# First output projection by column halves, with decay exponents as differences of running totals, in a three-block model on one core

## The reference

```python
proj = h @ w_in                      # q, k, v, g_a, z, xbc, dt_raw
y_a = rmsnorm(diff_attention(q, k, v), subln_w) * silu(g_a)
dt = softplus(dt_raw + dt_bias)      # 512 tokens x 16 heads
dA = dt * -exp(a_log)                # in 4 chunks of 128 tokens
cs = cumsum(dA, axis=-1)             # running total within the chunk
lmat = exp(where(l >= s, cs[l] - cs[s], -inf))
cb = einsum('bclgn,bcsgn->bcgls', cc, bc)
y_diag = einsum('bcgjls,bcsgjp->bclgjp', cb * lmat, xdt)
states = einsum('bclgn,bcgjl,bclgjp->bcgjpn', bc, exp(cs[-1] - cs), xdt)
h = h * exp(cs[-1]) + states         # scan over the chunks
y_off = einsum('bclgn,bcgjpn,bcgjl->bclgjp', cc, h_before, exp(cs))
y_b = rmsnorm_by_groups((y_diag + y_off + xh * d_skip) * silu(z))
x = x + concatenate([y_a, y_b], -1) @ w_out
```

## Time and profile before

| | |
|---|---|
| Median of 3 runs | 1669.97 us (1668.33 to 1672.4) |
| The profiled execution | 1672.1 us, of it 1670.2 us span |
| Mean granted TensorE clock | 0.976 |
| Busy: PE, DVE, ACT, POOL | 1575.8, 808.7, 655.9, 244.5 us |
| Rounds, first to last matmul of L1419 to L1455 | 358.17 to 430.1 us |
| Output projection, first product to the transposes of the next norm | 451.58 to 541.32 us |

### The profile page before, as it was taken

How to read it: one execution, slowest core, us unless ns; L and a number is a source line. 1 busy time by engine, 2 the same in 40 slices (tenths; PEclk the granted TensorE clock), 3 DMA queues, 4 the chain that set the end, 5 groups by cost and what they waited for, 6 DMA issues and landing times. The chain is left out here.

```text
span 1670.2 us, 20830 instructions
## 1 busy us (share of the span) xinstructions
PE 1575.8 (94%) x7924; PEld 1287.3 (77%) x7924; DVE 808.7 (48%) x1600; ACT 655.9 (39%) x1324; POOL 244.5 (15%) x148
## 2 busy tenths in 40 slices
PE   7999999899799999998999999988998999999997
PEld 6888777687687879877878777767776888887886
DVE  4222288746723655526723477726654433333224
ACT  4222355552512467625235454453244322222212
POOL 0000022267400011120002223221200000000000
PEclk9999999999899999999999999988999999999999
DMA  5232211111232431122431221112220322322232
GB/s 203 101 102 88 89 51 51 39 51 47 80 101 77 132 102 39 39 84 87 141 96 64 89 70 57 51 52 76 89 76 26 101 90 100 101 89 92 96 100 76
DMA packets 39777, 137.60 MB, mean 82 GB/s; under 512 B 4928, under 2 KB 5312, under 8 KB 39552
## 3 DMA queue, kind: packets, MB, share of 16 engines
q1 hardware_dynamic: 34400, 125.32, 22.7%
q10 hardware_dynamic: 5280, 10.97, 2.2%
HBM read 128.02 MB, written 2.10 MB: 78 GB/s over the span
## 5 line engine op out<-in xcount | busy, mean ns | idle before, releaser
L210 ACT ACTIVATE cut_hi<-raw 128x1024 fp32r<-128x1024 f32 x228 | 241.6, 1060 | 646.8 <-PE ps L227 631.8
L227 PE MATMUL ps<-h_hi,cut_hi 128*128 128x512 f32 (+1 forms) x1120 | 453.0, 404 | 5.9 <-DVE h_lo L425 3.9
L215 DVE TENSOR_TENSOR cut_lo<-raw,cut_hi 128x1024 fp32r<-128x1024 f32 x172 | 211.8, 1231 | 492.0 <-ACT cut_hi L210 490.2
L229 PE MATMUL ps<-h_hi,cut_lo 128*128 128x512 f32 (+1 forms) x1120 | 438.1, 391 | 0.0
L228 PE MATMUL ps<-h_lo,cut_hi 128*128 128x512 f32 (+1 forms) x1120 | 437.8, 391 | 0.0
L227 PEld LDWEIGHTS ps<-h_hi,cut_hi 128*128 128x128 f32 x1120 | 212.5, 190 | 70.0 <-issue 22.9
L229 PEld LDWEIGHTS ps<-h_hi,cut_lo 128*128 128x128 f32 x1120 | 212.1, 189 | 45.6
L228 PEld LDWEIGHTS ps<-h_lo,cut_hi 128*128 128x128 f32 x1120 | 212.9, 190 | 37.6
L215 POOL TENSOR_TENSOR cut_lo<-raw,cut_hi 128x1024 fp32r<-128x1024 f32 x56 | 133.7, 2388 | 675.1 <-ACT cut_hi L210 675.1
L227 PE MATMUL ps<-cut_hi,h_hi 128*128 128x512 f32 (+1 forms) x368 | 143.4, 390 | 10.2 <-DVE cut_lo L215 6.4
L229 PE MATMUL ps<-cut_hi,h_lo 128*128 128x512 f32 (+1 forms) x368 | 142.5, 387 | 0.0
(11 more groups left out here) (312 smaller groups left out, 2103.3 us busy)
## 6 DMA issues: line engine op xcount, KB each, us to landing
raw<-weights SPq DMA_DIRECT2D x228, 512.0 KB, 3.3
scr<-scr ACTq DMA_DIRECT2D x34, 64.0 KB, 3.6
x<-x_in SPq DMA_DIRECT2D x4, 512.0 KB, 6.1
x<-x_in ACTq DMA_DIRECT2D x1, 2048.0 KB, 7.5
q_stack<-qT_lo ACTq DMA_DIRECT2D x16, 128.0 KB, 2.3
out<-x SPq DMA_DIRECT2D x4, 512.0 KB, 2.6
consts<-tables ACTq DMA_DIRECT2D x1, 1732.0 KB, 7.9
arena<-arena ACTq DMA_DIRECT2D x8, 128.0 KB, 2.3
```

The source lines that it names most:

```text
L210: act.activation(cut_hi[:, u % CUT, :], raw[:, u % RAW, :], ACT.Copy).then_inc(hi_ready, 1)
L215: eng.tensor_tensor(cut_lo[:, u % CUT, :], raw[:, u % RAW, :], cut_hi[:, u % CUT, :].bitcast(F32), ALU.subtract).then_inc(lo_ready, 1)
L227: a = pe.matmul(out, left[0], right[0], start=start, stop=False)
L229: return a, pe.matmul(out, left[1], right[0], start=False, stop=stop)
```

## The change

It has two parts, made together.

**Exponents.** POOL's `make_dstr` is gone. One more fp32 matmul (bank 4) gives the running total of every chunk and head as a row: 64 records (chunk, head) on the partitions, twice, 128 tokens along the row. ACT and DVE make of it `run_rows`, high parts on partitions 0 to 63, low parts on 64 to 127. `pick` is two identities above each other, so a matmul with one of its columns, broadcast to 128, copies one record's high plus low part onto all partitions. `segs` is now 8 such matmuls a round, both operands fp32r, 128 columns. `run_cols` holds the same totals as columns. ACT forms Relu(cs[s] - cs[l]) head by head (8 activations of 128 columns, bias a column of `run_cols`), then one Exp of 1024 columns with scale -1; entries above the diagonal become 1 and are zeroed by `cbm`. Banks 0 and 1 are free when the Relus have read them (`segs_read`). The two last state updates, whose results nobody reads, are left out (PE, POOL and DVE).

**Output projection.** The new part `OutA` replaces eight parts. A unit is now two input blocks by 512 columns; units 0 to 7 make the left half in banks 2, 3, 0, 1, units 8 to 15 the right half in banks 4 to 7. y_a is transposed through the four left banks in two passes, and the products of units 0 to 2 (all y_a) stand ahead of the transposes of y_b, which go through the right banks before units 3 and 4. The last two units are again interleaved by token tile.

```diff
-            pool.tensor_tensor(dstr[i % 2], const("tri_gt").unsqueeze(1).broadcast_to([P, 8, P]),
-                               dta[:, at_h:at_h + 8].unsqueeze(2).broadcast_to([P, 8, P]), ALU.mult)\
-                .then_inc(dstr_ready, 1)
...
+        run_rows = at("run_rows", [P, P], F32R, ARENA + 10752)
+        pick = at("pick", [P, 64], F32R, ARENA + 10752 + P)
+        dta_twice = arena[:, 11008:11136]
+        run_cols = small[:, 784:848]
...
+                pe.matmul(ps[:, 4, 0:P], dta_twice, const("tri_le"), start=True, stop=True).then_inc(decay_sums, 1)
...
...
                     dve.wait_ge(turned_x, i + 1)
...
+                dve.tensor_tensor(run_rows[64:128, :], ps[64:128, 4, 0:P], run_rows[64:128, :].bitcast(F32), ALU.subtract)\
+                   .then_inc(run_ready, 1)
                 dve.wait_ge(cb_done, 1)
                 for i in range(2):
...
-                    pe.wait_ge(dstr_ready, i + 1)
                     if i >= 1:
-                        pe.wait_ge(segs_exp, 2 * i)
+                        pe.wait_ge(segs_read, 2 * i)
...
                         last = pe.matmul(ps[:, j // 4, (j % 4) * P:(j % 4 + 1) * P],
-                                         dstr[i % 2][:, j, :], const("tri_le"), start=True, stop=True)
+                                         pick[:, 8 * i + j:8 * i + j + 1].broadcast_to([P, P]), run_rows[:, :],
+                                         start=True, stop=True)
                         if j % 4 == 3:
...
+                pe.wait_ge(run_ready, 2)
...
-                      .then_inc(st_done, 1)
+                    if i < 6:
...
+                        pe.matmul(ps[:, 6, :], b_tok[:, c, g * P:(g + 1) * P], xdd[i % 2], start=True, stop=True)\
+                          .then_inc(st_done, 1)
...
-                        act.activation(exps[i % 2][:, 4 * half:4 * half + 4, :],
-                                       ps[:, half, :].rearrange("p (i l) -> p i l", i=4), ACT.Exp)\
-                           .then_inc(segs_exp, 1)
...
+                            last = act.activation(exps[i % 2][:, j, :], ps[:, half, (j % 4) * P:(j % 4 + 1) * P], ACT.Relu,
+                                                  scale=-1.0, bias=run_cols[:, 8 * i + j:8 * i + j + 1])
+                        last.then_inc(segs_read, 1)
+                    act.wait_ge(segs_read, 2 * i + 2)
+                    act.activation(exps[i % 2], exps[i % 2], ACT.Exp, scale=-1.0).then_inc(segs_exp, 1)
                     if i in (0, 1, 3, 4, 5, 7):
                         gates.act_turn(act)
...
-                    if 1 <= i < 7:
-                        pool.wait_ge(segs_done, 2 * i)
-                        make_dstr(pool, i + 1)
...
-                        .then_inc(xdd_ready, 1)
+                    if i < 6:
...
                     dve.tensor_tensor(y, ps[:, 4 + 3 * (i % 2), :], y, ALU.add).then_inc(y_out, 1)
-                    if c > 0:
...
+            yb_turned, yb_hi_out, yb_lo_out = (sem("yb_" + m) for m in ("turned", "hi_out", "lo_out"))
...
+                for k, t in order:
+                    if w is None:
+                        w = unit(pe, self.u0 + v)
+                    y = [(h[:, k % 8, t * P:(t + 1) * P]) for h in ((h_hi, h_lo) if k < 8 else (yb_hi, yb_lo))]
+                    bank = (self.left, self.right)[half][t]
+                    if half == 0 and t == 0:
+                        pe.wait_ge(self.ya_lo_out if k < 8 else self.yb_lo_out, k % 8 + 1)
+                    if half == 0 and k == 0:
+                        pe.wait_ge(self.ya_gated, 4 + t + 1)
+                    if half == 1 and k == 0:
+                        pe.wait_ge(self.yb_lo_out, 4 + t + 1)
+                    a, z = product(pe, ps[:, bank, :], y, [h[:, (k % 2) * 512:(k % 2 + 1) * 512] for h in w],
+                                   k == 0, k == 15)
...
+            def pe(self, pe):
+                pe.wait_ge(sl_scaled, NT)
+                pe.wait_ge(fill_g.out_act, 8)
+                for k in range(4):
+                    if k == 2:
+                        pe.wait_ge(segs_read, 16)
+                    self.turn(pe, y_a, k, self.left[k], self.ya_turned)
+                for k in range(4, 8):
+                    pe.wait_ge(self.ya_gated, k - 3)
+                    self.turn(pe, y_a, k, self.left[k - 4], self.ya_turned)
+                for v in range(8):
+                    if v == 3:
+                        pe.wait_ge(gs_scaled, 5)
+                        pe.wait_ge(gs_scaled_act, 3)
+                        pe.wait_ge(off_read, 6)
+                        pe.wait_ge(y_out, 8)
+                        pe.wait_ge(st_out, 6)
+                        for k in range(4):
+                            self.turn(pe, y_b, k, self.right[k], self.yb_turned)
+                    if v == 4:
...
+                            pe.wait_ge(self.yb_lo_out, k - 3)
+                            self.turn(pe, y_b, k, self.right[k - 4], self.yb_turned)
+                    self.columns(pe, 0, v, [(k, t) for k in (2 * v, 2 * v + 1) for t in range(NT)])\
...
+                for v in range(8, 14):
+                    self.columns(pe, 1, v, [(k, t) for k in (2 * v - 16, 2 * v - 15) for t in range(NT)])\
...
+                for t in range(NT):
+                    first = self.columns(pe, 1, 14, [(12, t), (13, t)])
...
+                    first = self.columns(pe, 1, 15, [(14, t), (15, t)])
+                    if t == NT - 1:
+                        first.then_inc(weights_used, 1)
...
-                act.wait_ge(turn_a.turned, 8)
+                act.wait_ge(fill_g.out_act, 8)
+                for k in range(8):
+                    act.activation(gate_a[:, k, :], gate_a[:, k, :], ACT.Silu).then_inc(self.ya_silued, 1)
+                    if k == 3:
+                        squares_of(act, 6)
+                squares_of(act, 7)
+                for k in range(8):
+                    if k == 6:
+                        cut_high(act, self.u0 + 1)
+                    act.wait_ge(self.ya_gated, k + 1)
+                    act.activation(h_hi[:, k, :], gate_a[:, k, :], ACT.Copy).then_inc(self.ya_hi_out, 1)
+                act.wait_ge(self.ya_turned, 8)
...
-                pe.wait_ge(gs_scaled, 5)
-                pe.wait_ge(gs_scaled_act, 3)
...
+                cut_high(act, self.u0 + 2)
+                cut_high(act, self.u0 + 3)
+                for k in range(8):
+                    if k == 4:
+                        cut_high(act, self.u0 + 4)
+                    act.wait_ge(self.yb_turned, k + 1)
+                    act.activation(yb_hi[:, k, :], ps[:, self.right[k % 4], :], ACT.Copy,
+                                   scale=col("ssd_norm", k)).then_inc(self.yb_hi_out, 1)
+                for v in range(5, self.n):
+                    cut_high(act, self.u0 + v)
...
+                dve.scalar_tensor_tensor(gate_a[:, k, :], ps[:, self.left[k % 4], :], subln8, gate_a[:, k, :],
...
+            def dve(self, dve):
+                for k in range(4):
+                    self.gate(dve, k)
+                dve.wait_ge(sd_squared, 8)
+                dve.tensor_scalar(ms[:, 0:8], ss[:, 0:8], 1.0 / 512, EPS_A, ALU.mult, ALU.add).then_inc(gs_mean, 1)
+                for k in range(4, 8):
...
+                dve.wait_ge(gs_rooted, 1)
+                for i in range(5):
+                    dve.tensor_scalar(groups_b[:, i, :], groups_b[:, i, :], rs[:, i:i + 1], None, ALU.mult)\
+                       .then_inc(gs_scaled, 1)
+                    if i == 2:
+                        cut_low(dve, self.u0 + 1)
+                cut_low(dve, self.u0 + 2)
+                cut_low(dve, self.u0 + 3)
+                for k in range(8):
+                    if k == 4:
+                        cut_low(dve, self.u0 + 4)
+                    dve.wait_ge(self.yb_hi_out, k + 1)
...
+                for v in range(5, 9):
+                    cut_low(dve, self.u0 + v)
...
+                for t in range(NT):
+                    self.add(dve, 0, t)
+                for v in range(9, self.n):
+                    cut_low(dve, self.u0 + v)
+                for t in range(NT):
+                    self.add(dve, 1, t)
+                    self.after.beside(dve, t, 0)
+                    self.after.beside(dve, t, 1)
...
+            def pool(self, pool):
+                pool.wait_ge(gs_mean, 1)
+                pool.tensor_tensor(rs[:, 0:8], ms[:, 0:8], neg_half[:, 0:8], ALU.pow).then_inc(gs_rooted, 1)
...
+                    pool.wait_ge(self.ya_hi_out, k + 1)
+                    pool.tensor_tensor(h_lo[:, k, :], gate_a[:, k, :], h_hi[:, k, :].bitcast(F32),
+                                       ALU.subtract).then_inc(self.ya_lo_out, 1)
...
+    chunk(a["w_out_a"][0], 512, 2)
     w = a["w_in_c"][0]
```

(65 more changed lines are left out.)

98 lines of the change are left out of this document (39 added, 59 removed).

## The result

The changed kernel takes 1652.05 us (median of 4 runs, 1649.7 to 1653.38); the kernel before took 1669.95 us beside it (4 runs, 1668.33 to 1672.4). The ratio is 0.9891, with a 95% interval from 0.9877 to 0.9906: 17.9 us gained where 15 were forecast, and the time lies within the range. By that interval the gain is between 15.7 and 20.5 us. The profiled execution took 1651.32 us.

What follows compares the result with a forecast made beforehand. PE, busy in 94% of the span, was taken as the bound. The first product's 21.5 us (8.3 from the rounds) less 3.7, 2.25 and 0.3 gave 15.2: from the median 1669.97 to 1655 us, range 1650 to 1663.

Steps and rivals of the forecast that it cites:

- The picks and the settled round: `segs` in the rounds: eight fp32r matmuls take 0.9 us instead of 1.8, 7.2 us gained; settled round 8.5 instead of 9.43.
- POOL: Rounds: POOL writes no 128x1024 triangle any more, so PE's two waits for it go, 1.8 us gained.
- st of round 6: Rounds: leaving out this state matmul gains 0.86 us; that of round 7, behind the last y, gains nothing.
- The added matmul: Ahead of the rounds: one more fp32 matmul of 128 columns on PE, 0.23 us lost.
- ACT's latency in rounds 0/1: `segs(1)` needs all eight Relus of round 0, 3.1 us after `segs(0)`, now 2.73: 1.3 us off the sum.
- ACT's latency in round 7: Between `segs(7)` and the last y: Relus, Exp and mix take 4.9 us of 6.2, just covered, 1.3 to spare.
- The first product: Start of the projection, behind ACT's squares, mean, POOL's root and one low half: 430.1 instead of 451.58, 21.5 us.
- Given back in the projection: Inside the projection: transposes of y_b 3.7 us, low clock 2.25, longer chain of the last tile 0.3.
- B's slow picks: Rival in the rounds: broadcast column loaded or multiplied at fp32's pace, 6.3 us less; 1659 to 1663, chance 0.18 (including ACT's pace).
- C's starving: Rival in the projection: units 1 to 3 cut late, 1.5 us each, clock rises slower; 1660 to 1662, chance 0.12.
- D: Rival for the whole kernel: slower than before because the clock stays at 1.2 GHz; 1675 and up, chance 0.03.
- E: Rival for the whole kernel: no difference, the first product's gain taken back; chance 0.05, of which 0.03 within 0.3%.

Runs made afterwards that it cites:

- early_pick: Changed kernel with the first eight picks issued ahead of five filler turns instead of behind them; 1646.82 us, ratio 0.9865 to the kernel before.
- relus_twice: Changed kernel with each half's four Relus done twice into the same place; 1653.57 us in one run.
- picks_fp32: Changed kernel with the picks multiplied as fp32 instead of fp32r; 1653.65 us in one run.
- both_early: Changed kernel with both reorderings, those of early_pick and early_gate; 1646.10 us, ratio 0.9864 to the kernel before.
- early_gate: Changed kernel with ACT's first high half of y_a between the Silus and POOL's first low half ahead of the root; 1648.26 us, ratio 0.9879 to before.

## Why the prediction was right, point by point

- *The picks and the settled round*: right. 8.5 us forecast, 8.54 measured; eight picks take 358.06 - 357.22 = 0.84 us, forecast 0.9. From the 81 ns of the Trainium skill (TensorE: Matmul & The Clock Gate, Back-to-back issue gap) an estimate would be 0.65 and the round 8.3; the trace does not agree, and stays at the 0.11 us of the earlier trace rows.
- *POOL*: right, and a little more. PE's waits for POOL are gone. The two rounds that had them are shorter from y to y by 11.04 - 8.54 = 2.50 and 10.18 - 8.51 = 1.67 us; without the 0.9 of the picks in each that is 2.4 us, forecast 1.8.
- *st of round 6*: half right. From y of round 6 to y of round 7 it was 427.32 - 423.11 = 4.21 us and is 419.80 - 416.06 = 3.74: 0.47 gained, forecast 0.86, as the off of round 7 now waits for DVE's read behind the mix.
- *The added matmul*: 0.23 forecast. From L1346 to the scores before it was 0.69 us, and is now 352.36 - 351.39 = 0.97: 0.28.
- *ACT's latency in rounds 0/1*: the mechanism right, the size off. Forecast: `segs(1)` waits about 2 us where it waited 0.78, 1.3 off the sum. The new wait is 1.81 us, 1.0 more than the old one, and as early_pick shows the clock behind it costs 1.7: 2.7 off the sum. This is the term that was mis-sized: the prediction charged the clock only to the projection. The last y ends 7.5 us earlier (421.53 against 429.05) instead of 8.3: 1.4 lost here and 0.4 at the st of round 6, against 0.6 won at POOL's waits and 0.4 in smaller steps.
- *ACT's latency in round 7*: right for ACT, whose Exp ends 0.8 us before DVE takes up the mix; but DVE's read behind the mix holds the off up by 0.3 us, which the prediction didn't have. relus_twice shows 2.5 us of wait there when ACT is late.
- *The first product*: 430.1 forecast, 430.37 measured, in part by luck: the last y ended 0.8 us later than forecast (421.53, not 420.7), and the mean hung on DVE's gates (427.2) where ACT's squares (426.8) were named as the later. From the mean on the chain is as told. From Y to the first product the gain is 24.26 - 10.57 = 13.7 us, forecast 21.5 - 8.3 = 13.2.
- *Given back in the projection*: the transposes of y_b 3.7 forecast; each 16 of them hold the next product off by 1.67 us (448.31 to 449.98), 3.3 in all. The clock: 17.94 us from the first product to the transposes at 448.31, where 24 products at 0.682 are 16.4: 1.6 instead of 2.25. The tail: nothing instead of 0.3; from the start of the last product's last matmul to N it is 1.17 us in both kernels (524.01 and 540.15 to N). In all 94.81 - 89.74 = 5.1 us from the first product to N, forecast 6.25.
- *Rivals*: B's slow picks are refuted by the 8.54, and picks_fp32 shows that they would have cost 5 us. C's starving didn't occur in the changed kernel; both_early and early_gate show it at once (1.9 us at unit 1) when the products come 2.3 us earlier, as the sum of spare time said. That the spare time vanishes if the clock doesn't fall didn't come true: in picks_fp32 it didn't fall and no unit waited. D and E didn't come about either.
- *The sum*: 15.2 forecast, 16.3 and 15.0 in the marks (without the 0.28 of the added matmul), 17.9 in the medians. That it comes so near is in part luck: from S to Y 7.7 us were gained where the terms give 8.5, from Y to N 8.6 where they give 13.2 - 6.25 = 6.95. The medians hold 1 to 3 us that the marks don't explain; since N to the end moves by 11 us between profiles of one kernel, I leave them open.

## What to carry to other kernels

When PE is busy 95% of the time, look for the point where it waits for a chain of other engines, and put products there that need nothing of that chain: that was 6.5 of the projection's 8.6 us. A wait of PE can cost more than itself: 1.8 us of waiting brought 1.7 us of half-speed matmuls, in another profile 3.3, though 1.37 us in picks_fp32 brought none. So when the order of two stages is open, issue early what starts the longest latency (here eight picks, 3.6 us for a reordering). To compare two profiles of a long kernel, lay marks around the changed part and don't read the span.

## What was not expected of the hardware

- A stretch of 1120 us of unchanged code took from 1117.5 to 1128.9 us in twelve profiles; in the two of the kernel before the clock's loss, as estimated above, accounts for it. Single executions of the kernel before lie between 1660.86 and 1672.4 us, the medians of its four sets between 1668.44 and 1669.95.
- After the wait of 1.8 us in the first rounds the low clock lasted differently from profile to profile: the rounds took 67.44 us in one of the changed kernel and 69.07 in the other. The first product, 10.57 and 10.56 us behind Y, met a low clock in the one and a full one in the other (0.77 and 0.47 us for its first matmul).
- DVE's low cut of 1024 columns took 2.31 us while POOL wrote low halves beside it, against 1.23 at 444.44 us with POOL idle; and POOL's eight low halves took 12.89 us, against 10.78 in the kernel before. That the two engines slow each other is not shown by a run of its own.
